# A modulation matrix read by row blocks and multiplied on VectorE and TensorE, overlapped mixer heads and three banks for attention's output tiles, in a fused network kernel on one Trainium2 core

## The reference, cut to what matters

```python
cond = jax.nn.silu(c)
for l in range(DEPTH):                      # DEPTH = 2
    mod = cond @ ada_w[l] + ada_b[l]
    shift, scale, gate = jnp.split(mod, 3, axis=-1)
    h = rms_norm(x, norm_g[l]) * (1.0 + scale[:, None, :]) + shift[:, None, :]
    y = even_mixer(h, ...) if l % 2 == 0 else odd_mixer(h, ...)
    x = x + gate[:, None, :] * y
```

## Time and profile before

| | |
|---|---|
| median of 3 runs | 3014.02 us (3010.43 to 3016.37) |
| profiled execution, own time | 3013.56 us |
| its span | 3012.0 us |
| TensorE busy | 2799.3 us, 93% of the span |
| TensorE's weight loads | 2337.7 us, 78% |
| VectorE busy | 1507.9 us, 50% |
| ScalarE busy | 898.3 us, 30% |
| GpSimd busy | 237.1 us, 8% |
| mean granted clock of TensorE | 0.969 |
| moved by DMA | 268.04 MB, 89 GB/s on average |

### The profile page before, as it was taken

The page is one execution under the profiler, slowest core; times in us unless marked ns, Lnnn a source line. Parts: engine busy times, 40 slices in busy tenths (PEclk is TensorE's granted clock), DMA queues, the critical chain, the costliest instruction groups (busy, mean ns, idle before and its releaser), DMA issues.

```text
span 3012.0 us, 33602 instructions
## 1 busy us (share of the span) xinstructions
PE 2799.3 (93%) x14398; PEld 2337.7 (78%) x14398; DVE 1507.9 (50%) x1798; ACT 898.3 (30%) x1209; POOL 237.1 (8%) x172
## 2 busy tenths in 40 slices
PE   4769979989899999999899999999999999899998
PEld 4657768766588888787788888888897888788886
DVE  5357675445444445453644446444446535544445
ACT  1223335544332222434322223222222222232221
POOL 2276630001000000000000000000000000000000
PEclk9679989999999999999999999999999999999999
DMA  8033421111243232222323333333232222143230
GB/s 262 26 106 102 117 70 43 55 49 66 56 125 100 84 100 82 71 70 71 112 84 93 109 92 98 100 109 86 98 109 70 85 70 84 56 126 98 84 111 29
DMA packets 329312, 268.04 MB, mean 89 GB/s; under 512 B 10250, under 2 KB 309516, under 8 KB 328908
## 3 DMA queue, kind: packets, MB, share of 16 engines
q1 hardware_dynamic: 325932, 254.02, 28.1%
q0 software_dynamic: 2512, 8.68, 0.8%
q10 hardware_dynamic: 720, 3.19, 0.3%
HBM read 263.76 MB, written 2.10 MB: 88 GB/s over the span
## 4 chain that ended last, share of the span: by engine, by line
PE 83%; DVE 11%; ACT 2%; issue 2%; POOL 1%; DMA 1%; SPq 0%; DVEq 0%; ACTq 0%; POOLq 0%
PE psum L305 15%; PE psum L307 15%; PE psum L306 15%; PE psum L372 7%; PE psum L374 7%; PE psum L373 7%; PE psum L349 3%; PE psum L351 3%; PE psum L350 3%; DVE w_lo L298 2%; DVE acc L452 1%; PE psum L2124 1%; DVE stat L601 1%; DVE acc L611 1%; DVE acc L614 1%
## 5 line engine op out<-in xcount | busy, mean ns | idle before, releaser
L305 PE MATMUL psum<-h_hi,w_hi 128*128 128x512 f32 (+1 forms) x2248 | 848.2, 377 | 31.9 <-DVE h_lo L564 18.6
L307 PE MATMUL psum<-h_hi,w_lo 128*128 128x512 f32 (+1 forms) x2248 | 832.5, 370 | 0.0
L306 PE MATMUL psum<-h_lo,w_hi 128*128 128x512 f32 (+1 forms) x2248 | 832.4, 370 | 0.0
L298 DVE TENSOR_TENSOR w_lo<-w_raw,w_hi 128x2048 fp32r<-128x2048 f32 x176 | 414.7, 2360 | 256.5 <-ACT w_hi L293 248.3
L305 PEld LDWEIGHTS psum<-h_hi,w_hi 128*128 128x128 f32 x2248 | 430.5, 192 | 106.7 <-issue 34.0
L307 PEld LDWEIGHTS psum<-h_hi,w_lo 128*128 128x128 f32 x2248 | 429.7, 191 | 71.4
L306 PEld LDWEIGHTS psum<-h_lo,w_hi 128*128 128x128 f32 x2248 | 430.5, 191 | 69.5 <-issue 3.1
L452 DVE SCALAR_TENSOR_TENSOR acc<-psum,acc 128x512 f32<-128x512 f32 x424 | 286.7, 688 | 208.9 <-PE psum L374 208.8
L293 ACT ACTIVATE w_hi<-w_raw 128x2048 fp32r<-128x2048 f32 x176 | 334.3, 1907 | 80.7 <-PE psum L374 32.0
L785 DVE SCALAR_TENSOR_TENSOR f_hffn<-f_sffn,psum 128x512 f32<-128x512 f32 x88 | 60.6, 688 | 507.4 <-ACT f_sffn L753 507.4
L753 ACT ACTIVATE f_sffn<-psum 128x512 f32<-128x512 f32 x88 | 52.6, 598 | 688.7 <-PE psum L307 688.7
(11 more groups left out here) (341 smaller groups left out, 3673.0 us busy)
## 6 DMA issues: line engine op xcount, KB each, us to landing
w_raw<-in_ffn_w_in SPq DMA_DIRECT2D x176, 512.0 KB, 5.3
w_raw<-in_ffn_w_out SPq DMA_DIRECT2D x88, 512.0 KB, 4.5
w_raw<-in_ret_w_in SPq DMA_DIRECT2D x48, 512.0 KB, 4.6
w_raw<-in_odd_w_in SPq DMA_DIRECT2D x32, 512.0 KB, 5.0
ada_first<-in_ada_w SPq DMA_DIRECT2D x12, 1024.0 KB, 11.2
w_raw<-in_even_w_in SPq DMA_DIRECT2D x24, 512.0 KB, 6.8
ada_raw<-in_ada_w SPq DMA_DIRECT2D x24, 512.0 KB, 4.0
w_raw<-in_gla_w_in SPq DMA_DIRECT2D x24, 512.0 KB, 4.9
```

Source lines behind the costliest of these rows:

```text
L298: k.nc.vector.tensor_tensor(k.lo(n), k.w_raw[:, buffer(n), :], k.hi(n).bitcast(F32), SUB).then_inc(*k.up("w_lo", n))
L305: k.nc.tensor.matmul(out, ws, xs, start=first, stop=False)
L306: k.nc.tensor.matmul(out, ws, xl, start=False, stop=False)
L307: return k.nc.tensor.matmul(out, wl, xs, start=False, stop=last)
```

## The change

The first layer's matrix is read in two parts. Its shift and scale columns come as eight row blocks of 128 x 2048 (rows of 8 KB, 1024 KB a block) into a ring of four; blocks 0, 2, 3, 5, 6 are multiplied by one number per partition and summed up on VectorE over all 2048 columns, blocks 1, 4, 7 are multiplied on TensorE, 16 calls each, and 16 calls sum VectorE's result over the partitions; a reduction on VectorE adds the four parts. `c` and the first 256 columns of the tables are loaded first, each by itself, and GpSimd's queue issues the small vectors' loads. The gate columns (8 blocks of 128) and the second layer's 24 blocks are all multiplied on TensorE (`tensor_ada`, 8 calls a block): four and four in head 0 before its levels, then six a head in the first six level steps. `gpsimd_first` and `gpsimd_ada` are gone.

In the even mixer v is projected wide with g, copied out by ScalarE and turned by four transposes; the square, the sum, the pooling, the root, the products and the splits of a head are moved into the next head's projections, with banks of their own (`TAIL_BANKS`); the last head writes its splits to buffers of their own (`e_oh_hi`, `e_oh_lo`) and its sum and pooling stand behind the third output tile. The next head's `qf` piece is issued between the third and the fourth `ada` block. The gate is spread in level steps 3 and 5 of head 0.

In attention the output tiles take banks 0, 1, 7 in turn, VectorE adds them earlier, the root of the slot before stands ahead of the second exponential, and in slot 7 the eight additions of the third output piece stand ahead of a weight piece.

```diff
+BY_TENSOR = (1, 4, 7)
+BY_VECTOR = tuple(n for n in range(KD) if n not in BY_TENSOR)
...
+def sync_start(k):
+
     sp, a = k.nc.sync, k.a
+    sp.dma_start(k.crow, a["c"].rearrange("b (j p) -> (b j) p", p=P)).then_inc(*k.up("c", 0, 16))
+    for n in range(KD):
+        if n >= RING:
+            sp.wait_ge(*first_free(k, n - RING))
+        sp.dma_start(k.first_w[:, n % RING, :], a["ada_w"][0][n * P:(n + 1) * P, 0:2 * D]
+                     ).then_inc(*k.up(f"first{n % RING}", n, 16))
+    sync_piece(k, AT["even", "qf", 0])
+    sync_piece(k, AT["even", "vg", 0])
+    sp.dma_start(k.consts[:, 2 * P:], a["consts"][:, 2 * P:]).then_inc(*k.up("tables", 0, 16))
+    sp.wait_ge(*k.at("vrow_zero", 0))
+    for at in (0, 32, 64):
...
+    po.wait_ge(*k.at("vrow_zero", 0))
...
+        po.dma_start(k.vrow[at:at + n, :], m).then_inc(*k.up("vec", 0, 16))
...
+    if n == BY_VECTOR[0]:
+        ve.tensor_scalar(x, w, k.cond[:, n:n + 1], None, MULT).then_inc(*k.up("first_rows", n))
...
+        ve.scalar_tensor_tensor(x, w, k.cond[:, n:n + 1], x, MULT, ADD).then_inc(*k.up("first_rows", n))
...
+def tensor_first(k, m):
+
+    pe, n = k.nc.tensor, BY_TENSOR[m]
+    pe.wait_ge(*k.at(f"first{n % RING}", n))
+    for j in range(16):
+        ins = pe.matmul(first_column(k, m, j), k.first_w[:, n % RING, j * P:(j + 1) * P], k.cond[:, n:n + 1],
+                        start=True, stop=True)
...
+    pe.wait_ge(*k.at("c", 0))
+    pe.wait_ge(*k.at("consts", 0))
+    pe.matmul(k.bank[1][:, 0:KD], k.crow, k.ident[0:KD, 0:KD], start=True, stop=True).then_inc(*k.up("c_turned", 0))
+    pe.wait_ge(*k.at("cond", 0))
+    tensor_first(k, 0)
     pe.wait_ge(*k.at("vec", 0))
-    pe.wait_ge(*k.at("consts", 0))
-    for g in range(2):
-        ins = pe.transpose(k.bank[0][:, g * P:(g + 1) * P], k.vrow[:, g, :], k.ident)
...
+    tensor_first(k, 2)
+    pe.wait_ge(*k.at("first_rows", BY_VECTOR[-1]))
+    for j in range(16):
+        ins = pe.matmul(first_column(k, 3, j), k.first_sum[:, j * P:(j + 1) * P], k.ones[:, 0:1], start=True, stop=True)
+    ins.then_inc(*k.up("first_cols", "sum"))
...
+    for n in BY_VECTOR[:3]:
+        vector_first(k, n)
+    ve.wait_ge(*k.at("consts", 0))
     for t in range(NT):
         vector_modulated_tile(k, "even", t)
-    for n in range(BY_COLUMNS, FIRST):
-        if not by_gpsimd(n):
-            vector_first(k, n)
+    for n in BY_VECTOR[3:]:
+        vector_first(k, n)
+    ve.wait_ge(*k.at("vcol", 0))
+    vector_lower(k)
+    vector_lower_sum(k)
+    mod = k.mod[:, 0, 0:16]
+    ve.wait_ge(*k.at("first_cols", "sum"))
+    ve.tensor_reduce(mod, k.bank[7][:, 0:64].rearrange("p (m j) -> p j m", j=16), AX, ADD).then_inc(*k.dve.up())
+    ve.wait_ge(*k.dve.at())
+    ve.tensor_tensor(mod, mod, k.vc("ada_b", 0, 16), ADD).then_inc(*k.up("mod", (0, "scale")))
...
+def sync_ada(k, n):
+    sp, (l, at) = k.nc.sync, (0, 16 + n) if n < KD else (1, n - KD)
     if n >= AR:
         sp.wait_ge(*k.at("ada", n - AR))
...
+        for n in range(n_vg if i else n_ub, n_ub + 1):
+        blocks = range(0 if i == 0 else KD + 6 * i, KD + 6 * i + 6)
+        for n in blocks:
+            if n == blocks[AR] and not late:
+                sync_piece(k, AT["even", "qf", i + 1])
+            sync_ada(k, n)
...
-def gpsimd_ada(k, i, j):
...
-    po.tensor_tensor(w3, w3, k.cond[:].unsqueeze(2).broadcast_to((P, KD, P)), MULT).then_inc(*k.pool.up())
-    for half in (512, 256):
-        po.wait_ge(*k.pool.at())
-        po.tensor_tensor(w[:, 0:half], w[:, 0:half], w[:, half:2 * half], ADD).then_inc(*k.pool.up())
-    po.wait_ge(*k.pool.at())
-    if j == 0:
...
+def tensor_ada(k, n, col):
+
+    pe = k.nc.tensor
+    pe.wait_ge(*k.at(f"ada_in{n % AR}", n))
+    for kk in range(KD):
+        ins = pe.matmul(col, k.ada_raw[:, n % AR, kk * P:(kk + 1) * P], k.cond[:, kk:kk + 1], start=kk == 0,
+                        stop=kk == KD - 1)
+    ins.then_inc(*k.up("ada", n))
...
+            project_half(k, S, n_vg, 0, (bk[2], bk[3]), range(0, KD // 2))
             tensor_turn_tile(k, S, 3, STREAM[S])
+            project_half(k, S, n_vg, 0, (bk[2], bk[3]), range(KD // 2, KD))
+            project_half(k, S, n_qf, 1, (bk[0], bk[1])).then_inc(*k.up("used", n_qf))
+            project_half(k, S, n_vg, 1, (bk[2], bk[3])).then_inc(*k.up("used", n_vg))
+            for n in range(KD // 2):
+                tensor_ada(k, n, k.bank[0][:, n:n + 1])
+        else:
+            pe.wait_ge(*k.at("e_u", i - 1))
+            pe.wait_ge(*k.at("e_gb_silu", i - 1))
+            if i == 1:
+                pe.wait_ge(*k.at("gate", (S, 1)))
+                pe.wait_ge(*k.at("mod", even_mod(0)))
+            project_pair(k, n_qf, 0, 1).then_inc(*k.up("used", n_qf))
+            tensor_even_sum(k, i - 1)
+            tensor_even_pool(k, i - 1)
             pe.wait_ge(*k.at("w_lo", n_vg))
-            pe.wait_ge(*k.at("mod", (0, "scale")))
-            tensor_even_values(k, n_vg, 0, bk)
-            project_half(k, S, n_qf, 1, (bk[0], bk[1])).then_inc(*k.up("used", n_qf))
-            for n in range(BY_COLUMNS, FIRST):
-                tensor_first(k, n, 3)
-            tensor_even_values(k, n_vg, 1, bk).then_inc(*k.up("used", n_vg))
-            tensor_spread(k, 0, (0, 1), [("h_lo", (S, 1, 3))] * 2)
-        else:
-            pe.wait_ge(*k.at("e_gb", i - 1))
-            project_pair(k, n_qf, 0, 1).then_inc(*k.up("used", n_qf))
-            pe.wait_ge(*k.at("w_lo", n_vg))
-            pe.wait_ge(*k.at("e_rs", i - 1))
-            for t in range(NT):
-                ins = project_tokens(k, n_vg, k.bank[2][:, t * P:(t + 1) * P], t, 0, P)
-            ins.then_inc(*k.up("e_v_done", i))
-            pe.wait_ge(*k.at("mod", even_mod(i - 1)))
-            project_one(k, n_vg, 1, 3).then_inc(*k.up("used", n_vg))
...
+            if m == 0:
+                if n_out is not None:
+                    pe.wait_ge(*k.at("acc", (n_out, 5)))
+                elif i:
+                    pe.wait_ge(*k.at("e_root", i - 1))
+            if m < 6:
+                tensor_ada(k, KD + 6 * i + m, k.bank[bk[5]][:, m:m + 1])
+            if i == 0 and m in (3, 5):
+                tensor_even_spread(k, (m - 3) // 2)
...
+    i, n = NH - 1, AT[S, "out", NH - 2]
+    pe.wait_ge(*k.at("w_lo", n))
+    for c in range(2):
+        pe.wait_ge(*k.at("oh_lo", (S, i - 1, c)))
+    free = [("e_rs", i - 1), ("mod", even_mod(i)), ("e_keep", (i, KD - 2)), ("e_keep", (i, KD - 1))]
+    for j in range(8):
+        pe.wait_ge(*(k.at(*free[j]) if j < 4 else k.at("acc", (n, j - 4))))
+        for c in (1, 0):
+            ins = out_part(k, n, j, c, c == 1, c == 0, k.oh_hi, k.oh_lo)
+        ins.then_inc(*k.up(*out_done(n, j)))
+        if j == 2:
+            tensor_even_sum(k, i)
+            tensor_even_pool(k, i)
...
+        if i:
+            scalar_even_root(k, i - 1)
...
+        sc.wait_ge(*k.at("used", n_vg))
+        sc.activation(k.s_E[:, 1, :], bank[2], ACT.Copy).then_inc(*k.up("e_v_raw", i))
+        if i:
+            scalar_even_split(k, i - 1)
...
+            vector_even_pooled(k, i - 1)
...
+        if i:
+            vector_even_out(k, i - 1)
...
+        if i:
+            vector_even_split(k, i - 1)
...
+            if i == 0 and m == 1:
+                vector_even_gate(k)
+        vector_ada(k, i)
+    i = NH - 1
+    vector_even_pooled(k, i)
+    vector_piece(k, AT[S, "out", i - 1])
+    vector_piece(k, AT[S, "out", i])
+    for j in range(3):
+        vector_out(k, AT[S, "out", i - 1], j)
+    vector_even_gb(k, i)
+    vector_even_out(k, i)
+    for j in (3, 4):
+        vector_out(k, AT[S, "out", i - 1], j)
+    vector_even_split(k, i)
+    for j in (5, 6, 7):
+        vector_out(k, AT[S, "out", i - 1], j)
     vector_modulated(k, "odd")
     vector_piece(k, HEAD["odd"][0])
     vector_piece(k, HEAD["odd"][1])
...
-OUT_BANK = (0, 1, 0, 1, 7, 0, 1, 7)
...
-OUTS_AT = ((0,), (1, 2), (3, 4), (5,), (6, 7))
+OUT_BANK = (0, 1, 7, 0, 1, 7, 0, 1)
...
+OUTS_AT = ((0, 1), (2, 3), (4, 5), (6,), (7,))
...
-        elif j < 4:
-            pe.wait_ge(*k.at("acc", (n, j - 2)))
-        elif j == 4:
+        elif j == 2:
...
         if 0 < p < 7:
             scalar_gated(k, p - 1)
+        if p:
+            scalar_fill_root(k, SLOT_FILL[p - 1][3])
         scalar_exp(k, p, 1)
-        if p:
-            scalar_fill_root(k, (SLOT_FILL[p - 1] + [None] * 4)[3])
...
+        if p == 7:
+            vector_out_tiles(k, fill[2], range(8))
         vector_filled(k, p, 1, fill)
         if p == 7:
-            vector_out_tiles(k, fill[2], range(8))
             vector_gated_rest(k, 6)
```

More of the change, by code:

```diff
@@ L1104, in gpsimd_even @@
         n_qf, n_vg, n_ub, n_out, late = even_pieces(i)
[L1105 to L1106 removed]
         if n_out is not None:
             gpsimd_gate(k, n_out)
[L1109 to L1110 removed]
+        po.wait_ge(*(k.at("e_pool", i - 1) if i else k.at("h_lo", ("even", 1, 3))))
+        po.dma_start(k.s_pw, k.a["pool_w"][0][i]).then_inc(*k.up("e_pw", i, 16))
         for n in range(len(LEVELS)):
```

(18 more changed lines are left out.)

409 lines of the change are left out of this document (172 added, 237 removed).

## The result

The changed kernel takes 2934.0 us (median of 4 runs, 2932.18 to 2939.71) against 3012.22 for the kernel before in the same series (3009.11 to 3016.37): 0.9742 of it, with an interval of 0.973 to 0.9753. The forecast was 2941 in a range of 2905 to 2980. Its profiled execution took 2933.21 us with a span of 2931.9, 80.1 less than the span before.

What follows compares the result with a forecast made beforehand. TensorE was taken to bound the kernel, with holes in the start, heads and attention slots 4 and 7. Terms 27.5 + 26.3 + 6.6 + 0.5 + 12.5 = 73.4 us gave 2941 us, range 2905 to 2980.

Steps and rivals of the forecast that it cites:

- The start: Ahead of the first projection: from 82 to about 54.5 us, 27.5 us earlier, bounds 21 to 33.
- rival 4: In the start, VectorE's 2.3 us instructions hold the small vector loads, TensorE's block 4 behind them: 2956 us; chance 0.04.
- Head 0: Head 0's stretch falls from 121.3 to about 95 us, 26.3 in the sum; bounds 18 to 33.
- Heads 1 and 2: The two heads together fall from 146.8 to 140.2 us, net 3.3 a head.
- Head 3: Head 3 with the exit goes from 86.5 to 86 us; bounds minus 5 to plus 6.
- 2.6 less at the end, where the outputs' first tiles run while the pooling is made: At head 3's exit, TensorE starts output tiles during the pooling, saving 2.6 us.
- Attention: Attention takes 12.5 us less through banks, earlier additions and ScalarE's earlier root; bounds 3 and 22.
- With banks 0, 1, 7 in turn tile 3 needs tile 0, tile 4 tile 1: In attention's slot 4, the bank order removes the shorter of two waits on acc, 3.9 us.
- Rival 5: In attention, the third bank only moves the wait to tile 7, so attention gives 2 us: 2951; chance 0.07.
- (1): In the level steps the clock does not hold; if half of them fall, 2981 or 2966 us; chance 0.13.
- (2): All level steps in all heads run at 0.50 and the start gives its least: slower, 3050 us; chance 0.03.
- (3): One-column matmuls hold the clock in the start, gate blocks and steps: 21 us less, 2920; chance 0.07.

Runs made afterwards that it cites:

- experiment 3: Three runs of the changed kernel with one-column blocks dealt anew: eight in head 0's steps; two of these earlier; one a step throughout. 2946.99, 2934.76, 2925.45 us.

## Why the prediction was right, and where it was not

**The start** (27.5 meant, 23.7 measured). VectorE's blocks at 2.35 us and a TensorE block at 6.96 us came as priced, and behind block 1 TensorE waited for no block. Block 1 itself was through at 17.3 us and not at 23, and the wait for the small vectors took that up. The step that failed is rival 4's "They should be issued by 10 us, before the second block": they were issued in time, and I took issued for landed. Block 4 began at 28.4 instead of 25, which is 3.4 us of the 3.8 missing; the tiles took 1.0 more, and block 7 with the summing calls 11.1 where 12 was meant. The clock, by the two groups of profiles, decides over another 3 us. Rival 4 named the right wait with the wrong cause, and put it 10 us too late.

**Head 0** (26.3, 28.2). The projections took 28.0 us (29.0 meant), the gate blocks 25.2 (24.4 meant). The step "the first two blocks at 1.68 and the other six at 3.5" is nearly what the windows show: 21 instructions at the full rate where it means 32. The levels with the values took 36.7 us where 38.3 was meant, since one step ran at half clock and not one and a half; the others held 1.00.

**Heads 1 and 2** (6.6, 8.7). 69.2 and 68.9 us where 70.1 was meant; the wait at the third output tile is 0.75 us, not 1.1.

**Head 3** (-0.5, +1.6). The 3.7 us for `w_lo` of ub are 4.1, the gates cost 2.6 where 1.7 was meant. The step that failed is "2.6 less at the end, where the outputs' first tiles run while the pooling is made": they could not start, since ScalarE made their `w_hi` only behind the square. And the forecast priced no clock behind that hole: the next 12 matmuls took 5.28 us, at a clock row of 0.50, and would have taken 2.8 at the 0.23 us that they need later (my estimate).

**Attention** (12.5, 20.3; the bounds were 3 and 22). The step that failed is "With banks 0, 1, 7 in turn tile 3 needs tile 0, tile 4 tile 1", from which the forecast lets the shorter wait go: it went because VectorE adds tiles 1, 3, 5 and 6 one place earlier, an edit that the forecast did not price. Nor did the 2.3 us for slot 7's additions ahead of the weight piece come: without that move slot 7 takes the same 40.1 us. The 1.5 us for the root are another error: the number came true by luck, at attention's first half, by the clock. Rival 5 was right of the bank and wrong of the time.

**The rivals of the clock.** (1) and (2) fell by head 1's row of 1.00; experiment 3 shows how near they were. (3) fell at 88.3 us, with the clock row at 0.58 on a busy TensorE.

**The signs.** The first projection at 58.25 us is just outside of the 50 to 58 that the forecast named, slots 4 and 7 (40.0 and 37.8 us) are below its 42 to 44, and a block in the levels takes 1.84 and not 1.7. GpSimd is busy for 93.7 us and not "under 60"; TensorE does not wait for it, except through the VectorE instructions that its gates stretch (the 2.6 us above).

**The sum.** That it came to within 7 us is in part luck. Attention's 7.8 us are nearly the whole miss. The start and head 3 gave 5.9 us less than forecast, and head 0, heads 1 and 2 and the rest 4.8 more, for reasons of their own.

## What to carry to other kernels

When tiles pass through a few banks, price the place of the instruction that frees them before the number of banks: here the one was worth 18 us over two slots and the other about 1, and the banks alone made one slot worse. Ask of a small load what stands ahead of it in its queue, since its issue time says nothing. One-column matmuls in a row fell to half of the clock here, and one block a step between wide ones kept it, so deal them out thinly, and not in runs.

## What was not expected of the hardware

- 24 KB issued behind 2048 KB from the same queue landed 18.9 us after the issue, and 5.7 when issued ahead of them.
- TensorE without idle time ran at 0.50 under one-column matmuls: 64 instructions in 13.65 us. With one block (16 instructions) in each step of head 1 the row reads 1.00; with two blocks a step in head 0, 0.62 and 0.66 in two runs.
- The clock row reads 1.00 over block 1 in the start, where the 32 instructions are spaced as at 0.50.
- The moment at which the pace rises in the start differs between executions, and moves the first projection by 3 us.
- VectorE's 128 x 2048 subtraction took 4.68 us where a GpSimd multiplication ran beside its first 2.5 us, and 2.28 without.
